# A transformer stack on one NeuronCore: how the two expert stages are entered (spare blocks, ring of weight slots, order of expert 0's work, gather, logits)

## What is computed

```python
def _expert_choice_ffn(u, w_router, w_g, w_u, w_d):
    cap = CAPACITY_FACTOR * n // N_EXPERTS          # 32 of 256 tokens
    logits = jnp.einsum('bnd,de->ben', u, w_router)
    aff = jax.nn.softmax(logits, axis=1)
    gate, idx = lax.top_k(aff, cap)
    xe = u[bidx, idx]
    hg = jnp.einsum('becd,edf->becf', xe, w_g)
    hu = jnp.einsum('becd,edf->becf', xe, w_u)
    ye = jnp.einsum('becf,efd->becd', jax.nn.silu(hg) * hu, w_d) * gate[..., None]
    return jnp.zeros_like(u).at[bidx, idx].add(ye)
```

## Time and profile before

| | |
|---|---|
| median of three executions | 2496.44 us |
| the profiled execution, its own time | 2500.81 us |
| its span, first to last instruction | 2499.0 us |
| mean granted clock of PE | 0.890 of full |
| read from device memory | 756.01 MB, 303 GB/s over the span |
| PE, DVE, ACT busy | 82%, 45%, 21% of the span |
| expert stage of layer 0, about | 1331 to 1835 us |
| expert stage of layer 1, about | 1972 to 2480 us |

### The profile page before, as it was taken

One profiled execution on the slowest core, in us unless ns is written; L12 is line 12 of the kernel. 1 busy time (PEld: TensorE's weight loads), 2 busy tenths in 40 slices (PEclk: granted clock), 3 DMA queues, 4 the chain that ended last, 5 costly groups with the idle time before them and its releaser, 6 DMA issues.

```text
span 2499.0 us, 33192 instructions
## 1 busy us (share of the span) xinstructions
PE 2040.7 (82%) x12372; PEld 1298.7 (52%) x12372; DVE 1119.0 (45%) x1724; ACT 528.3 (21%) x860; POOL 65.0 (3%) x96
## 2 busy tenths in 40 slices
PE   6998988998999898899996777777669676666664
PEld 4997455997899444899864311111148332111111
DVE  3886676888788666788543200000022320000002
ACT  3333133343433132433241100000010110000000
POOL 1000000000000000000200000000000000000000
PEclk7999998999999899999997977777779798888887
DMA  9986765888588664988624999999994579999996
GB/s 339 324 299 251 277 228 177 294 290 315 193 317 297 212 235 177 320 302 286 221 93 157 374 410 410 410 410 410 410 346 152 202 279 410 410 410 410 410 410 261
DMA packets 289373, 758.07 MB, mean 303 GB/s; under 512 B 17616, under 2 KB 125424, under 8 KB 289184
## 3 DMA queue, kind: packets, MB, share of 16 engines
q1 hardware_dynamic: 282368, 737.34, 78.5%
q0 software_dynamic: 6688, 19.78, 2.4%
q10 hardware_dynamic: 256, 0.13, 0.0%
HBM read 756.01 MB, written 1.18 MB: 303 GB/s over the span
## 4 chain that ended last, share of the span: by engine, by line
PE 54%; DMA 21%; SPq 13%; DVE 6%; issue 3%; ACT 2%; DVEq 1%; ACTq 0%
PE psum L727 21%; DMA W<-in_w_exp_up 16%; SPq L510 12%; PE psum L739 10%; PE psum L767 5%; PE psum L788 4%; PE psum L1127 3%; DMA W_mod<-in_mod_w 3%; PE psum L1065 3%; DMA W<-in_w_exp_down 1%; PE psum L963 1%; PE psum L700 1%; ACT uT L1173 1%; SPq L514 1%; PE psum L1077 1%
## 5 line engine op out<-in xcount | busy, mean ns | idle before, releaser
L727 PE MATMUL psum<-parts 128*128 128x256 f32 x4224 | 528.2, 286 | 15.0 <-DVE parts L1584 7.7
L727 PEld LDWEIGHTS psum<-parts 128*128 128x128 f32 x4224 | 525.7, 195 | 22.5 <-issue 16.3
L1065 PE MATMUL psum<-W,scr 128*32 128x512 f32 x1984 | 307.9, 721 | 163.1 <-DMA W<-in_w_exp_up 158.2
L1460 DVE SCALAR_TENSOR_TENSOR mod_acc<-W_mod,cond,mod_acc 128x1024 f32<-128x1024 f32 x196 | 251.8, 1285 | 50.7 <-issue 28.2
L1966 DVE TENSOR_TENSOR scr<-scr,psum 128x256 f32<-128x256 f32 x32 | 13.5, 422 | 576.8 <-ACT scr L1410 576.8
L739 PE MATMUL psum<-parts 128*128 128x512 f32 x1056 | 257.8, 394 | 0.0
L1065 PEld LDWEIGHTS psum<-W,scr 128*32 128x32 f32 x1984 | 49.1, 117 | 394.4 <-DMA W<-in_w_exp_up 332.5
L1584 DVE TENSOR_TENSOR parts<-W,parts 128x1024 fp32r<-128x1024 f32 x176 | 207.1, 1219 | 57.2 <-ACT parts L1203 57.2
L1090 PE MATMUL psum<-W,scr 128*32 128x256 f32 x2048 | 168.2, 475 | 65.7 <-DMA W<-in_w_exp_down 50.6
L739 PEld LDWEIGHTS psum<-parts 128*128 128x128 f32 x1056 | 192.7, 188 | 45.1 <-DVE parts L1597 8.2
L1203 ACT ACTIVATE parts<-W 128x1024 fp32r<-128x1024 f32 x176 | 175.8, 1051 | 46.4 <-issue 46.4
(11 more groups left out here) (291 smaller groups left out, 1663.7 us busy)
## 6 DMA issues: line engine op xcount, KB each, us to landing
W<-in_w_exp_down SPq DMA_DIRECT2D x128, 1024.0 KB
W<-in_w_exp_gate SPq DMA_DIRECT2D x248, 512.0 KB, 15.0
W<-in_w_exp_up SPq DMA_DIRECT2D x248, 512.0 KB, 15.7
W_mod<-in_mod_w SPq DMA_DIRECT2D x123, 1024.0 KB, 5.0
W<-in_ffn_w_gate SPq DMA_DIRECT2D x44, 1024.0 KB, 9.4
W<-in_ffn_w_up SPq DMA_DIRECT2D x44, 1024.0 KB, 11.9
W<-in_ffn_w_down SPq DMA_DIRECT2D x44, 1024.0 KB, 9.2
W<-in_w_in SPq DMA_DIRECT2D x24, 1024.0 KB, 8.4
```

The lines of the kernel that those rows point to most:

```text
L727: ins = pe.matmul(psum[:, 4 + t % 2, S * g:S * g + S], w[:, t % 2, g, kc, :], u[:, kc, :], start=(n == 0 and kc == 0), stop=(n == 2 and kc ...
L1065: ins = pe.matmul(psum[32 * q:32 * q + 32, 4, :].rearrange("p (g n) -> p g n", g=2), xe_now[:, kc, :], w[:, :, q, :], start=(kc == 0), sto ...
L1460: ins = dve.scalar_tensor_tensor(acc[:, :], w, col, acc[:, :], mul, add)
```

## The change

It touches the expert stages and what lies ahead of them.

- Six spare tiles instead of four, for blocks 0 to 5 of expert 1. The new ones are `k_mixer`, one tile that holds the first mixer's constants, and `gate_att`, one tile for `gate_row` and `att_0`. Spares 0, 1, 2 (`k_mixer`, `wm0`, `qm`) are asked for before the mixer's end: in layer 0 after `p12`, `pool1` and `S15`, in layer 1 after the convolution's `f7`. Spares 3 and 4 (`gate_att`, `tmp`) wait for the norm, spare 5 (`uT`) for the logits.
- From expert 1 on, block b lies in slot (b - 6) mod 8: blocks 6 and 7 of expert 1 go into slots 0 and 1 after `k0` and `k1` of expert 0, blocks 0 to 5 of expert 2 into slots 2 to 7 after `k2` to `k7`.
- POOL's gate row in layer 0's and layer 1's expert stage waits for `k3` of expert 1, with what stands behind it on POOL.
- The logits of tile 0 are computed before tile 1 is transposed; ACT signals its evacuations of tile 0 in pairs. The logits lie in PSUM bank 0.
- The first selection and gather take two experts (`FEW` = 64 columns) instead of four; the other 448 columns follow.
- In expert 0 PE computes the down product before most of the second gather, and the addition to the output after expert 1's gate and up.
- DVE's `plus_bias` comes after expert 2; `e_out` and `e_set` are semaphores of their own in place of two steps.

The core of the diff (ACT and DVE are reordered in the same way as PE):

```diff
-SPARE = 4
+SPARE = 6
+FEW = 2 * CAP
...
-                fills[s] += units - (2 if phase.startswith("moe") and s < SPARE else 0)
+                fills[s] += units - (2 if phase.startswith("moe") and KC - SPARE <= s < KC else 0)
+        def ring_slot(b):
+            return (b - SPARE) % KC
...
+            def ring_block(layer, e, b, used, E):
+                sp.wait_ge(e_pe.s, e_pe.at(f"k{used}", E))
+                s = ring_slot(b)
+                gate_up_block(layer, e, b, W[:, s, :], landed[s])
...
+            def expert_stream(layer):
+                E0 = EXPERTS * layer
+                for b in range(SPARE, KC):
+                    ring_block(layer, 1, b, b - SPARE, E0)
+                for b in range(SPARE):
+                    ring_block(layer, 2, b, b + KC - SPARE, E0)
+                for q in range(4):
+                    ring_down(layer, 1, q, E0)
+                for b in range(SPARE, KC):
+                    ring_block(layer, 2, b, b, E0 + 1)
+                for q in range(4):
+                    ring_down(layer, 2, q, E0 + 1)
...
+            def late_spares(layer):
+                spare_slots(layer, [(b, (pn_x, 2 * (6 + 2 * layer) + 4)) for b in (3, 4)] + [(5, (r_pe.s, r_pe.at("logits", layer)))])
+            first_slots(0, [(s, (pe_down, 1 + FFN_TILES)) for s in (9, 10, 11)])
+            first_slots(0, [(s, m2_done("p12")) for s in MIXIN_S])
+            spare_slots(0, [(0, m2_done("p12")), (1, m2_done("pool1")), (2, m2_done("S15"))])
+            first_slots(0, [(s, m2_done("out")) for s in MIXOUT_S])
+            late_spares(0)
+            expert_stream(0)
...
+            first_slots(1, [(s, (cv_pe.s, cv_pe.at(f"f{2 * (s // 3) + 1}"))) for s in range(4, SLOTS)])
+            spare_slots(1, [(b, (e_pe.s, e_pe.at(f"k{b}", 1))) for b in range(3)])
+            first_slots(1, [(s, (cv_pe.s, cv_pe.at("out"))) for s in range(4)])
+            late_spares(1)
+            expert_stream(1)
...
+                if s in (7, 9):
+                    pool.wait_ge(e_pe.s, e_pe.at("k3", EXPERTS * (s // 2 - 3) + 1))
                 pool.dma_start(gate_row[:, :], mod_rows[ds(row, 1), :].to_broadcast([P, D])).then_inc(rows_landed, 16)
...
                 for t in range(TT):
+                    turn_tile(15 + 4 * layer + t, t)
+                    if t:
+                        turned(10 + 2 * layer)
                     for kc in range(KC):
+                        if t == 0:
+                            turned_first(10 + 2 * layer, kc)
-                        ins = pe.matmul(psum[:, 4, EXPERTS * t:EXPERTS * t + EXPERTS], uT[:, kc, P * t:P * t + P],
+                        ins = pe.matmul(psum[:, 0, EXPERTS * t:EXPERTS * t + EXPERTS], uT[:, kc, P * t:P * t + P],
...
-                        ins = pe.matmul(psum[:, kc, 0:P], x_tok[:, t, P * kc:P * kc + P], sel[:, t, 0:P],
+                        ins = pe.matmul(psum[:, kc, 0:FEW], x_tok[:, t, P * kc:P * kc + P], sel[:, t, 0:FEW],
...
+                gate_up(0, first=True)
+                gates_turned()
+                pe.wait_ge(r_dve.s, r_dve.at("rest", layer))
+                gather_rest(0)
+                hidden_turned(0)
+                gather_rest(1)
+                down(0, first=True)
+                for kc in range(2, KC):
+                    gather_rest(kc)
+                gate_up(1, extra=True)
+                added(0, first=True)
+                expert_end(1)
                 with pe.Fori(2, EXPERTS) as e:
-                    expert(e, False)
+                    gate_up(e)
+                    expert_end(e)
```

More of the change, by code:

```diff
@@ L140 @@
 CONSTS = ("ident", "ones", "later", "strict", "decay", "windows", "closed", "rope1")
+MIXER_ONLY = ("later", "strict", "decay", "windows", "closed", "rope1")
 CONSTS2 = ("pool", "w_grp", "rope2", "qk_gain", "p_scale", "w_router", "conv_w", "slot_no")
@@ L379, in expert_landed @@
         def expert_landed(layer, s, e, first):
-            return e * 32 + (slot_landed(f"moe{layer}", s) - (32 if s < SPARE and not first else 0))
+            return e * 32 + (slot_landed(f"moe{layer}", s) - (32 if KC - SPARE <= s < KC and not first else 0))
         block = ctx.enter_context(nc.Block())
@@ L517, in slot_use @@
[L517 to L536, removed]
-                with sp.Fori(3, EXPERTS) as e:
-                    for s in range(SLOTS):
-                        sp.wait_ge(e_pe.s, e_pe.at(slot_use(s), e + (EXPERTS * layer - 1)))
-                        expert_slot(layer, e, s)
@@ new lines, in down_block, with first_slots @@
+            def down_block(layer, e, q):
+                sp.dma_start(part(W[:, KC + q, :], 0, 2, D), A["w_exp_down"][layer, ds(e, 1), 256 * q:256 * q + 256, :]
+                             .rearrange("a (k p) n -> p (a k) n", p=P)).then_inc(landed[KC + q], 32)
+            def first_slots(layer, waits):
+                for s, (sem_, n) in waits:
+                    sp.wait_ge(sem_, n)
+                    if s < KC:
+                        gate_up_block(layer, 0, s, W[:, s, :], landed[s])
+                    else:
+                        down_block(layer, 0, s - KC)
@@ new lines, in expert_stream @@
+            def expert_stream(layer):
[10 more added lines that the diff above has]
+                    ring_down(layer, 2, q, E0 + 1)
+                with sp.Fori(3, EXPERTS) as e:
+                    for b in range(KC):
+                        ring_block(layer, e, b, b, e + (E0 - 1))
+                    for q in range(4):
+                        ring_down(layer, e, q, e + (E0 - 1))
@@ L1083, in expert, with down @@
                     ins.then_inc(e_pe.sig("hT"), 1)
-                    pe.wait_ge(e_act.s, e_act.at("hT", E))
+                def down(e, first=False):
+                    pe.wait_ge(e_act.s, e_act.at("hT", e + EXPERTS * layer))
                     for c in range(KC):
@@ L1094, in expert, with added @@
                             ins.then_inc(e_pe.sig(f"d{c // 2}"), 1)
+                def added(e, first=False):
+                    E = e + EXPERTS * layer
                     pe.wait_ge(e_act.s, e_act.at("R", E))
@@ L1956, in experts, with tokens_and_gates @@
                 dve.drain()
-                def expert(e, first):
-                    E = e + EXPERTS * layer
+                def tokens_and_gates(e):
                     dve.tensor_copy(xe_now[:, :, :], xeT[:, :, ds(e * CAP, CAP)])
```

216 lines of the change are left out of this document (129 added, 87 removed).

## The result

The changed kernel takes 2472.78 us (median of 4, 2472.23 to 2480.42) beside 2497.43 us of the kernel before on the same chip: ratio 0.9904 [0.9888, 0.9919], 24.7 us saved where 29.9 were forecast. The profiled execution took 2472.23 us, span 2470.4. The 4.6 us are no gain of the change.

What follows compares the result with a forecast made beforehand. Each expert stage was taken as a weight stream at 409 GB/s; 7.7 + 1.4 + 4.8 = 13.9 us in layer 0 and 7.7 + 3.6 + 4.7 = 16.0 in layer 1 gave 29.9 us, so 2466.5, range 2457 to 2479.

Steps and rivals of the forecast that it cites:

- (b): Transfers' rest between the mixer-end burst and the resume in expert 0: 1.4 us shorter in layer 0, 3.6 in layer 1.
- (c): Transfers' rest until expert 0's down product frees a slot: goes, gaining 4.8 us in layer 0, 4.7 in layer 1.
- Rest (a): Transfers' rest before the mixer's last product ends, 35.5 and 21.5 us: three spare blocks hidden there, 7.7 us a layer.
- The margins of the turned ring: In expert 1, k6 comes 1.9 us and d0 0.2 us before the transfer queue needs them.
- R2: k6 of expert 1 or the d0 after it misses the queue's end: 3 to 5 us a layer, 2474; chance 0.14.
- R3: PE's clock stays up over the early logits: 2.5 us a layer faster, 2461.5; chance 0.14.
- R4: PE at 1.2 GHz through all of experts 0 and 1, queue dry some 27 us: slower, 2525; chance 0.03.
- R5: The blocks moved ahead of the mixer's end don't pay: about the rests alone, 14 us, 2482; chance 0.05.
- the small gather: First gather, streaming 64 columns instead of 128: gains nothing; bounds 1.5 us lost and 2.7 us won.
- R1: Clock rises late: first gather 1.5 us more, gate-up's k0 0.9 us later; 2.4 us a layer, 2471.3; chance 0.17.
- Blocks ahead: Three spare blocks asked for before the mixer ends take 7.7 us of transfers out of the time after it, each layer.
- my 7.5 us for the resume: After the burst, transfers resume on k0 of expert 0: 3.5 us plus 4.0 us from its earlier start.

Runs made afterwards that it cites:

- the last version: Changed kernel with first gather of 128 columns, POOL's columns early and unused products (8, 4, 4, 22, 3) on PE from the mixer's end: 2461.28 us, ratio 0.9843.

## Why the prediction was right and wrong

**Right in sign, in range and in what bounds the stage:** the expert stage is a stream, and its end is moved by rests of the transfers behind the mixer's end, (b) and (c). Rest (a) is not where time came from (below). The margins of the turned ring held: SP's issue on k6 of expert 1 comes at 1389.96, 31.0 us after expert 0's start (forecast: k6 done at +29.9, needed by +31.8), and no window from 1367.4 on shows a rest. R2, R3 and R4 did not happen (for R3: tile 1's half of the logits took 3.57 us). R5's time did not come either, though its premise, that the moved blocks don't pay, is half true: moved in time they paid nothing, as two blocks more they did. The logits gained 3.4 us (forecast 3.2), the select now takes 0.36 instead of 1.29 us (0.9 gained, forecast 0.8), the burst ends some 6.3 us sooner (forecast 6.1), the columns in the stream cost 2.3 us (forecast 2.2). One agreement is luck: the profiled span fell by 28.6 us beside a forecast of 29.9, but 4.6 us of that lie ahead of the change. The last down blocks came 25.2 us earlier in both layers together, which is what the medians show (24.7) and 4.7 us short of the sum.

**The step that failed in size is the small gather's.** I took "nothing", "as nearest to the logits' row", and gave R1 a chance of 0.17. R1 is what happened, in both of its terms. The gather costs 7.09 us, 1.56 more than the one of 128 columns (R1: 1.5), because all 32 instructions ran at 1.2 GHz (granted clock 0.50 from 1345.90 to 1361.00, above); gate-up starts at that clock, so SP's issue on k0 comes 1.98 us after gate-up's start where I reckoned 1.0 (R1: 0.9 later). R1's sum was 2.4 us a layer, 11.5 and 13.6 us; the last down blocks came 11.2 and 14.05 us earlier. The gather of 128 showed it from the other side. The row I called nearest, the logits at 218 ns an instruction, gave 7.0 us, and I had it in hand as a bound: I should have seen that both rows it was weighed against differ in clock only, and that the 128-column gather's 5.53 us held a rise of the clock that nothing assured to a gather of half the columns. The section on LDWEIGHTS in "TensorE: Matmul & The Clock Gate" of the Trainium skill has the time of a load follow the columns of the stationary operand. The rows here agree, all with loads of 128 columns: at 1.2 GHz 222 ns an instruction with 64 streamed columns and 218 with 16, at 2.4 GHz 120 ns with 128 (3.84 us for 32) and 120 with 16 (1.93 us for 16, in the last version).

**The step that failed in its reason is "Blocks ahead".** It said the three blocks asked for early take 7.7 us of work out of the time behind the mixer. They do, and the experiment with the spares behind the mixer shows it to be worth nothing: the burst is over 7.6 us before transfers resume even with all ten blocks in it. I called the 7.7 us a gain of their own, which would be lost with rest (a) ("they would cost their 7.7 us again"). With the blocks behind the mixer nothing was lost. The sum is not hurt by this, and not by luck: rest (b)'s term took off the 2.56 us by which the shorter burst lets the rest begin earlier, and 7.7 less 2.56 us is the worth of two blocks more. The count was sound, the reason put to its largest term was not. The account that the runs bear out leaves rest (a) out. At the resume 18 blocks have landed instead of 16: 2 x 2.56 = 5.1 us. The resume comes 5.4 us earlier in layer 0 and 5.8 in layer 1. The third rest is gone: 4.8 and 4.7 us. POOL's row and, in layer 0, its columns move into the stream: 3.6 and 1.3 us lost. Together 11.7 and 14.3 us, measured 11.2 and 14.05. With my 7.5 us for the resume the same account gives 13.8 and 16.0, my forecast. The kernel whose ring is not turned checks this account without the resume, which there stands 0.2 us behind that of before: the other terms give 6.1 and 8.3 us, and its last down blocks come 6.3 and 8.8 us earlier than before's. So the time at which the spare blocks were asked for did not count; that their number did is this account's reading, with no run of its own.

**Rest (c) was put down to two things, and one did it.** The step had the down slots freed before the eight blocks are through and ended the rest by both together. The eight blocks alone end it; moving the down product up changes no time while they are there (+0.2, -0.2 us). Whether it would be worth something without the turned ring was not tried.

**What stays open.** From 3 us after the resume the changed kernel moves, in two windows of 2.5 us in layer 0, 229 and 357 GB/s, though SP has blocks to issue; the kernel with the ring not turned moves 393 and more there. That is some 1.4 us. The version with 128 columns and 26 added products moves 411 and 418 there, but the one with the gather of 128 alone 267 and 328, though gate-up takes 7.07 us in both; so PE's rate is not the whole of it, and no run takes it apart. Open too is the difference of 1.2 us between last block and next stage's start in layer 0 (140.05 us, before 138.82), which lies within what the runs spread (138.3 to 141.7).

## What to carry to other kernels

Where a stage is one stream of weights, ask what has landed when the stream's queue first goes dry and when it is fed again: filling an earlier rest with blocks that would land in a later one anyway is worth nothing, and every microsecond ahead of the resume is worth nearly one. Before shrinking a product on TensorE, look at whether weight loads or streamed columns set its time, and at which clock the smaller one and all behind it will run. A try with idle TensorE time filled by products nobody reads is cheap where the path to the resume holds TensorE work: here it was worth 0.3 to 0.4% of the whole kernel with the gather of 128 columns, and 0.1%, which the noise covers, with that of 64.

## What the runs showed of the hardware

- TensorE's clock fell from 2.4 to 1.2 GHz while the engine was at work without a pause: in the 64-column gather (4.70 of 4.70 us busy) and in the 16-column logits (2.20 of 2.20 us busy) behind added products. In the 128-column gather it stayed at 1.00, behind much the same products and three more that left no pause ahead of it. For the logits it is no fixed thing: in the last version, with the same 8 and 4 products ahead of the halves, both halves ran at 1.00 in layer 0 (tile 1's in 1.93 us instead of 3.57), with 0.51 over the turn of tile 1 between them. What decides was not found.
- The gather of half the columns was the slower one: 7.09 against 5.53 us without added products; with them 6.04 and 4.65 (layer 0) against 3.84, where the three further products stand beside the columns as a difference. "TensorE: Matmul & The Clock Gate" of the Trainium skill, in its part on the clock gate, ties the full clock to TensorE being busy; the two falls above are rows of this case that this does not foretell.
- Four transfers of columns, issued by POOL from 1388.46 to 1391.98, took the transfers from 409 to 217 GB/s for 5 us with the DMA engines at full share; asked for ahead of the stage they left 408 and 410 GB/s in the same windows.
